# Head order, row transfers and mid-slot products in the scans of a hybrid encoder kernel

## The reference

```python
seg = a_cs[:, :, :, None] - a_cs[:, :, None, :]      # cumulative sums, position l minus position s
decay = jnp.exp(jnp.where(lower, seg, -jnp.inf))
cb = jnp.einsum('bclgn,bcsgn->bclsg', Cc, Bc)
y_diag = jnp.einsum('bclsge,bcsgep->bclgep', cb[..., None] * decay, X)
...
y_off = jnp.einsum('bclgn,bcgepn->bclgep', Cc, s_in) * jnp.exp(a_cs)[..., None]
return (y_diag + y_off).reshape(b, s, h, p)
```

## Time and profile before

| | |
|---|---|
| time, 3 runs | 1684.62 us median (1684.27 to 1687.24) |
| profiled execution: own time | 1684.64 us |
| profiled execution: span, first to last instruction | 1682.9 us |
| TensorE busy | 1659.0 us, 99% of the span |
| VectorE busy | 1001.9 us, 60% |
| GpSimd busy | 687.4 us, 41% |
| ScalarE busy | 679.8 us, 40% |
| granted TensorE clock | 1.00 (2.4 GHz) over the run |

### The profile page before, as it was taken

One profiled execution on the slowest core, in us unless ns is written; L12 is line 12 of the kernel. 1 busy time (PEld: TensorE's weight loads), 2 busy tenths in 40 slices (PEclk: granted clock), 3 DMA queues, 4 the chain that ended last, 5 costly groups with the idle time before them and its releaser, 6 DMA issues.

```text
span 1682.9 us, 20420 instructions
## 1 busy us (share of the span) xinstructions
PE 1659.0 (99%) x8004; PEld 1316.8 (78%) x8004; DVE 1001.9 (60%) x1387; ACT 679.8 (40%) x932; POOL 687.4 (41%) x339
## 2 busy tenths in 40 slices
PE   7999999999999999999999999999999999999999
PEld 5777787878778888888877777788777788888887
DVE  5589859778774545422236898596788654545100
ACT  5445553344443333332244555533543433333221
POOL 3432223233445555554443222232334455555443
PEclk9999999999999999999999999999999999999999
DMA  5532111212223232322224221112123223222233
GB/s 167 129 96 74 62 63 63 76 63 64 87 88 100 88 100 88 100 92 94 91 88 126 85 73 63 63 63 76 63 66 96 89 88 100 89 100 90 93 99 107
DMA packets 43231, 147.34 MB, mean 88 GB/s; under 512 B 5152, under 2 KB 5920, under 8 KB 43136
## 3 DMA queue, kind: packets, MB, share of 16 engines
q1 hardware_dynamic: 42752, 145.28, 26.9%
q0 software_dynamic: 384, 0.75, 0.4%
HBM read 143.17 MB, written 2.85 MB: 87 GB/s over the span
## 4 chain that ended last, share of the span: by engine, by line
PE 89%; DVE 6%; issue 2%; ACT 1%; POOL 1%; DMA 0%; SPq 0%; DVEq 0%
PE banks L1080 27%; PE banks L1082 26%; PE banks L1081 26%; PE banks L1172 2%; PE banks L1151 2%; PE banks L1160 2%; PE banks L1255 1%; DVE sb_w_lo L747 1%; PE banks L1268 1%; PE banks L1227 1%; PE banks L1131 1%; DVE sb_e L822 1%; PE banks L1241 1%; PE banks L1211 0%; DVE sb_squares L735 0%
## 5 line engine op out<-in xcount | busy, mean ns | idle before, releaser
L360 POOL TENSOR_TENSOR sb_w_lo<-sb_w_raw,sb_w_hi 128x1024 fp32r<-128x1024 f32 x202 | 490.4, 2428 | 633.1 <-ACT sb_w_hi L453 633.1
L1080 PE MATMUL banks<-sb_h_hi,sb_w_hi 128*128 128x512 f32 x1360 | 558.2, 410 | 16.1 <-POOL sb_w_lo L360 10.7
L453 ACT ACTIVATE sb_w_hi<-sb_w_raw 128x1024 fp32r<-128x1024 f32 x258 | 272.6, 1057 | 671.4 <-PE banks L1082 665.1
L1082 PE MATMUL banks<-sb_h_hi,sb_w_lo 128*128 128x512 f32 x1360 | 537.3, 395 | 0.0
L1081 PE MATMUL banks<-sb_h_lo,sb_w_hi 128*128 128x512 f32 x1360 | 537.1, 395 | 0.0
L1080 PEld LDWEIGHTS banks<-sb_h_hi,sb_w_hi 128*128 128x128 f32 x1360 | 256.5, 189 | 99.5 <-issue 36.9
L1081 PEld LDWEIGHTS banks<-sb_h_lo,sb_w_hi 128*128 128x128 f32 x1360 | 256.9, 189 | 61.8 <-issue 6.9
L1082 PEld LDWEIGHTS banks<-sb_h_hi,sb_w_lo 128*128 128x128 f32 x1360 | 256.5, 189 | 60.1
L1045 DVE TENSOR_TENSOR banks<-banks,sb_rstd 128x512 f32<-128x512 f32 x88 | 61.5, 699 | 144.0 <-PE banks L1082 135.7
L1080 PE MATMUL banks<-sb_ff_hi,sb_w_hi 128*128 128x512 f32 x352 | 138.9, 395 | 0.0
L1082 PE MATMUL banks<-sb_ff_hi,sb_w_lo 128*128 128x512 f32 x352 | 138.9, 395 | 0.0
(11 more groups left out here) (199 smaller groups left out, 2326.9 us busy)
## 6 DMA issues: line engine op xcount, KB each, us to landing
sb_w_raw<-w_in SPq DMA_DIRECT2D x88, 512.0 KB, 3.4
sb_w_raw<-w_up SPq DMA_DIRECT2D x88, 512.0 KB, 3.3
sb_w_raw<-w_out SPq DMA_DIRECT2D x32, 512.0 KB, 3.4
sb_w_raw<-w_down SPq DMA_DIRECT2D x32, 512.0 KB, 3.3
sb_bias_t<-bias_rows SPq DMA_DIRECT2D x16, 448.0 KB, 6.0
sb_w_raw<-w_down SPq DMA_DIRECT2D x16, 384.0 KB, 3.0
sb_x_stream<-x_t SPq DMA_DIRECT2D x4, 512.0 KB, 6.7
out_t<-sb_x_stream SPq DMA_DIRECT2D x8, 256.0 KB, 3.5
```

Of the source, the lines that this page charges most:

```text
L360: g.tensor_tensor(WLO[:, n % 2, :], W[:, n % 2, :], WHI[:, n % 2, :].bitcast(F32), ALU.subtract).then_inc(w_lo.handle, 1)
L453: sc.activation(WHI[:, n % 2, :], W[:, n % 2, :], ACT.Copy).then_inc(w_hi.handle, 1)
L1080: mm(out, whi, hhi, start=start, stop=False)
L1082: return mm(out, wlo, hhi, start=False, stop=stop)
```

## The change

The head's rows of cumulative sums no longer come from TensorE. ScalarE writes the sums and their exponentials (`exp_rows`) once a layer, SyncE stores both in DRAM (`store_rows`), and for every head a transfer spreads the two rows over 128 partitions straight into the head's tile (`head_rows`, 512 KB). Two transfers a pair fill `EA` (`pair_exps`, 2 x 192 KB), in place of ScalarE's L606. `seg` becomes eight instructions of 128 columns, each with a per-partition scalar, that subtract and limit at once, SBUF to SBUF. `CB` moves from SBUF into banks 2 and 3. The head tiles become four. GpSimd adds the directions for every head, so `within` has 8 matmuls. The tables change: the second group begins in slot 13; `SEG_AT` puts the first three heads of a group one to three slots behind its start and the others five to nine (before: three to ten); `WEIGH_AT` weighs them two to nine slots behind it; pairs stand in slots 7, 9, 11, 12 and 18, 20, 22, 24 (before 7, 9, 11, 13 and 19, 21, 23, 25), in the middle of the slot's matmuls except the fourth, which stays at its end, and `combine` follows `seg` in the slot, ahead of the slot's evacuation, except for the fourth. Two gates on GpSimd move a slot earlier or later.

```diff
-GROUP_AT = (2, 14)
-ROWS_AT = {GROUP_AT[h // 8] + 3 + h % 8: h for h in range(SSD_HEADS)}
-PAIR_AT = {GROUP_AT[t // 4] + 5 + 2 * (t % 4): t for t in range(SSD_HEADS // 2)}
+GROUP_AT = (2, 13)
+SEG_AT = {GROUP_AT[h // 8] + h % 8 + (1 if h % 8 < 3 else 2): h for h in range(SSD_HEADS)}
+WEIGH_AT = {GROUP_AT[h // 8] + 2 + h % 8: h for h in range(SSD_HEADS)}
+PAIR_AT = {GROUP_AT[t // 4] + 4 + 2 * (t % 4) + (t != 3): t for t in range(SSD_HEADS // 2)}
...
-    HEAD_E = (E[:, 0, :, :], E[:, 1, :, :], SQ[:, :, :])
+    HEAD_E = (E[:, 0, :, :], E[:, 1, :, :], rm["e_third"][:, :, :], SQ[:, :, :])
...
+    CB = BANK[:, 2:4, :]
...
+        def store_rows():
+            sp.wait_ge(*cs_row.at(1))
+            sp.dma_start(sum_rows[0, :, :], T[0:2 * DIR, 0, :]).then_inc(rows_stored.handle, 16)
+            sp.wait_ge(*cs_exp.at(1))
+            sp.dma_start(sum_rows[1, :, :], ER[0:2 * DIR, :]).then_inc(rows_stored.handle, 16)
+
+        def head_rows(h):
+            grp, n = h // 8, h % 8
+            if h == 0:
+                sp.wait_ge(*rows_stored.at(32))
+                sp.wait_ge(*at_pv.at(UNITS))
+            if n % 4 == 3:
+                sp.wait_ge(*st_mm.at(6 * grp + 6))
+            if h >= 4:
+                sp.wait_ge(*y_mm.at(2 * ((h - 4) // 2) + 2))
+            rows = bass.AP(sum_rows.tensor, h * SEQ, [[0, P], [DIR * SEQ, 2], [1, SEQ]])
+            sp.dma_start(head_e(h), rows).then_inc(rows_landed[h % 4].handle, 16)
+
+        def pair_exps(t):
+            if t >= 2:
+                sp.wait_ge(*y_read.at(t - 1))
+            for d in range(2):
+                rows = bass.AP(sum_rows.tensor, (2 * DIR + DIR * d + 2 * t) * SEQ + (P, 0)[d], [[SEQ, 2], [0, 64], [1, SEQ - P]])
+                sp.dma_start(EA[:, t % 2, d, :], rows).then_inc(ea_landed[t % 2].handle, 16)
...
+                slot = pos - POS["sc", 0]
+                if slot == 4:
+                    store_rows()
+                if slot - 2 in SEG_AT:
+                    head_rows(SEG_AT[slot - 2])
+                if slot - 1 in PAIR_AT:
+                    pair_exps(PAIR_AT[slot - 1])
...
-                if s in ROWS_AT and ROWS_AT[s] % 2 == 0:
-                    add_directions(ROWS_AT[s])
-                if s in PAIR_AT:
+                if PAIR_AT.get(s, 3) != 3:
                     add_backward(PAIR_AT[s])
+                if s in WEIGH_AT:
+                    add_directions(WEIGH_AT[s])
...
-                    act.wait_ge(*seg_read.at(h + 1))
-                    if h >= 4:
-                        act.wait_ge(*y_read.at(h // 2 - 1))
-                    sc.activation(EA[half, (h // 2) % 2, :, :].rearrange("p d l -> p (d l)"),
-                                  BANK[half, 2:4, :].rearrange("p b s -> p (b s)")[:, P:P + 768], ACT.Exp).then_inc(ea_done.handle, 1)
...
         def seg(h):
-            v.tensor_tensor(head_e(h).rearrange("p d (c l) -> p d c l", l=P),
-                            BANK[:, 2:4, :].rearrange("p d (c l) -> p d c l", l=P), columns, ALU.subtract).then_inc(seg_read.handle, 1)
-            dve.wait_ge(*seg_read.at(h + 1))
-            v.tensor_scalar(head_e(h), head_e(h), 80.0, None, ALU.min).then_inc(seg_done.handle, 1)
+            dve.wait_ge(*rows_landed[h % 4].at(16 * (h // 4 + 1)))
+            for d in range(2):
+                for c in range(QT):
+                    at = slice(P * c, P * c + P)
+                    ins = v.tensor_scalar(head_e(h)[:, d, at], head_e(h)[:, d, at], AS[:, c, column(d, h):column(d, h) + 1], 80.0,
+                                          ALU.subtract, ALU.min)
+            ins.then_inc(seg_done.handle, 1)
...
-        def row_sums(h):
...
-            for d in range(2):
-                ins = mm(bank(2 + d), SEL[:, column(d, h):column(d, h) + 1].to_broadcast([P, P]), CS[:, :], start=True, stop=True)
...
-                for h, d in ((2 * t, 0), (2 * t + 1, 0), (2 * t + 1, 1)):
+                for h in (2 * t, 2 * t + 1):
```

More of the change, by code:

```diff
@@ L233, in build_trunk @@
     x_stored = sem("x_stored")
-    sel_done, eps_done = sem("sel_done"), sem("eps_done")
+    eps_done = sem("eps_done")
+    rows_stored = sem("rows_stored", 32)
+    rows_landed = [sem(f"rows_landed{i}", 64) for i in range(4)]
+    ea_landed = [sem("ea_landed0", 128), sem("ea_landed1", 128)]
     bias_mm, bias_row = sem("bias_mm"), sem("bias_row")
@@ L270, in head_e @@
     def head_e(h):
-        return HEAD_E[h % 8 % 3]
+        return HEAD_E[h % 4]
     def par(col, n=1):
@@ L855, in state_in @@
                 return
-            if grp:
-                dve.wait_ge(*t_read.at(4))
+            dve.wait_ge(*(t_read.at(4) if grp else rows_stored.at(32)))
             col = 64 + column(d, 8 * grp)
@@ L954, in _ @@
                     dve.sem_inc(cs_col.handle, 1)
-                if s in ROWS_AT:
-                    seg(ROWS_AT[s])
+                if s in SEG_AT:
+                    seg(SEG_AT[s])
+                if PAIR_AT.get(s, 3) != 3:
+                    combine(PAIR_AT[s])
                 for grp in range(SSD_GROUPS):
@@ L1103, in block_of, with pair, between, tile @@
                 ins.then_inc(w_used.handle, 1)
-        def tile(kind, i, width=P, head=None):
+        def pair(s):
+            if s in PAIR_AT:
+                from_states(PAIR_AT[s])
+                within(PAIR_AT[s])
+        def between(s):
+            if PAIR_AT.get(s) != 3:
+                pair(s)
+        def tile(kind, i, width=P, slot=None):
             for k in range(KT):
-                if k == KT // 2 and head is not None:
-                    row_sums(head)
+                if k == KT // 2 and slot is not None:
+                    between(slot)
                 block_of(kind, i, k, width)
@@ L1270, in from_states, with output_first @@
             ins.then_inc(yo_mm.handle, 1)
-        def output_first(m, head):
+        def output_first(m, slot):
             s, b = weights("o1", m), tile_bank("o1", m)
             for k in range(KT):
-                if k == KT // 2 and head is not None:
-                    row_sums(head)
+                if k == KT // 2:
+                    between(slot)
                 at = slice(P * k, P * k + P)
@@ L1345, in _ @@
                 if kind == "o1":
-                    output_first(i, ROWS_AT.get(s))
+                    output_first(i, s)
                 else:
-                    tile(kind, i, head=ROWS_AT.get(s))
+                    tile(kind, i, slot=s)
                 if s == 0:
@@ L1364, in _ @@
                             chunk_state(6 * grp + 2 * (s - GROUP_AT[grp] - 1) + j)
-                if s in PAIR_AT:
-                    from_states(PAIR_AT[s])
-                    within(PAIR_AT[s])
+                if PAIR_AT.get(s) == 3:
+                    pair(s)
                 if s == 26:
```

78 lines of the change are left out of this document (26 added, 52 removed).

## The result

The changed kernel takes 1697.49 us (median of 4 runs, 1695.71 to 1698.76), the kernel before 1684.46 us in the runs beside it. The ratio is 1.0075, 95% interval 1.0062 to 1.0088: 13 us slower, where 1679 was forecast and 1695 was the upper end of the range.

What follows compares the result with a forecast made beforehand. TensorE (99% busy) was taken as the bound, VectorE close behind; of 17.1 us a layer new stalls left 2.9, 5.8 for two layers, from 1684.64 to 1679 us. Range 1658 to 1695; forecast alone 1674 to 1684.

Steps and rivals of the forecast that it cites:

- the 17.1 us that it can give: TensorE's most per layer: 7.5 us of row sums, 7.0 of products within chunks, 2.6 of stalls.
- A second term: Layer gain taken as 2.9 us, the middle between 0.5 by VectorE's list and 5.3 with `seg` at 1.2.
- The list itself: VectorE's work and waits followed through both groups' slots, with TensorE's resulting stalls: a layer wins 0.5 us.
- TensorE's side: In the scans: row sums gone, `within` about 1.02 us a pair, TensorE's busy share near 92%.
- VectorE's terms: For each head on VectorE: `seg` 1.6 us, `weigh` 1.2, and about 1.1 behind a GpSimd sum holding the port.
- The upper bound for `seg`, 1.8: Eight 128-column instructions on VectorE at 1.8 us, fixed part as in the 0.16 us of a one-column instruction.
- The stalls: TensorE idle for VectorE's low parts at slots 7, 11, 18 and 22, and before the fourth pair for GpSimd.
- The rows: Heads' row transfers land at 6.0 us, mostly hidden; VectorE waits 3 us at head 3 and head 11.
- The rival of late rows: Rows landing at 9.9 us lengthen waits at heads 3, 11, 5 to 7, 13 to 15: 1703; decides at 7.5; chance 0.14.
- The forecast's last sign of being wrong: The prediction is wrong if VectorE's waits in the scans are mostly for transfers.
- the 4.2 to 9.9 of the earlier trace: Landing times in us of the nearest recorded transfers, 448 KB bias transfers, median 6.0, taken for the heads' rows.
- The second forecast wait that mattered: First group's fourth pair: its products, ready at 313.7, wait for head 7's GpSimd sum at 317.7 and stand 4 us.

Runs made afterwards that it cites:

- runs with fillings: Matmuls nobody reads put before TensorE's long waits: on the changed kernel 1688.93 us; on the changed kernel with the three moves 1672.05 us.
- the third experiment: Changed kernel with row transfers of heads 3, 5, 7 and 11, 13, 15 asked for one slot earlier: 1685.5 us, 1.0006 against the kernel before.
- the three moves: Changed kernel with rows earlier, SiLU ahead of the head's exponential, head 7's (15's) sum ahead of the backward sum on GpSimd: 1681.15 us, 0.9983.
- the best run: The three moves on the changed kernel, plus matmuls nobody reads before four of TensorE's remaining waits: 1672.05 us, 0.9924 against the kernel before.

## Why the prediction was wrong

**The step that failed: that the gain of a layer is the 17.1 us that it can give, less the length of the new stalls.** The sum priced a stall at its own length, and all work at the clock of before, 1.00. The runs showed that a stall here costs its length and, mostly, a stretch at half clock behind it: 6.8 us in the first layer and 7.4 in the second, 14.3 us in all. No rival had it. Both runs with fillings show it directly: 8.6 us with the schedule as it was, 9.1 in the best one.

**A second term was too good.** The list itself gave 0.5 us a layer. The forecast took 2.9, half-way to the 5.3 that `seg` at 1.2 us would give (by its own terms, 0.5 and eleven times 0.4, that is 4.9). `seg` measured 1.58, so the 2.4 us a layer on top of the list, 4.8 in all, had no ground. The list alone says 1683.6; with the 14.3 us of the clock it is 1697.9, where 1697.5 was measured.

**TensorE's side held.** Row sums are gone, `from_states` takes 1.43 us and `within` 1.02 at full clock, as forecast. The busy share in the scans, forecast near 92%, is 88% and 92% in the two windows, slow matmuls counted as busy.

**VectorE's terms held.** `seg` 1.58 us (1.6), `weigh` 1.13 (1.2), a sum in front of `seg` or of the taps 1.03 (1.1). The Trainium skill, "SBUF — State Buffer", on who interferes with whom, has the pair of ports as an exclusive lock; the trace agrees also where the short instructions stand back to back: the 2.69 us above. The upper bound for `seg`, 1.8, was too high, and so was the estimate of the same size worked out from the Trainium skill, "VectorE: DVE Perf Modes", in the section on the TRN2 errata; the short instructions cost 0.20 us each, and eight less than the two long ones before.

**The stalls: the sum held, partly by luck; their places didn't all.** Forecast and measured in the first layer, us:

| | slot 7 | slot 11 | fourth pair | slot 18 | slot 22 | slot 24 | sum |
|---|---|---|---|---|---|---|---|
| forecast | 2.9 | 1.9 | 4.0 | 3.3 | 2.0 | 2.2 | 16.3 |
| measured | 2.73 | 1.41 | 4.63 (0.29 more for states) | 3.10 | 3.95 | 0 | 16.1 |

Slot 22 was delayed by head 13's rows, on top of SiLU: VectorE waited 3.94 us for them, its `seg` started at 386.24, ScalarE's exponential ended 2.7 us later, and SiLU, its tables and the high part followed. The part that wasn't in the forecast took that from slot 24. That the sums agree within 0.2 us is luck in part: rows came later than forecast, and with the rows on time (the third experiment) the same list of stalls is 11.5 us, 4.8 less than forecast.

**The rows: mechanism right, size and places off.** Waits were forecast at heads 3 and 11, 3 us each (3.53 and 2.69 measured). The rival of late rows put more at heads 5 to 7 and 13 to 15, from a landing at 9.9 us. The median is 5.3, so by its own condition (7.5) it didn't apply; yet single transfers land at 10, and 7.4 us of waits at heads 5, 7 and 13 came with them. The forecast had no term for the `EA` transfers that go out 5 to 9 us before these. The forecast's last sign of being wrong, VectorE waiting mostly for transfers, comes near: 13.6 us of VectorE's 35.3 us of waits in the two windows are for rows, more than for any other single cause. A landing is not one number: the 4.2 to 9.9 of the earlier trace rows was the better guide than its median.

**The second forecast wait that mattered was right in kind**: the fourth pair for GpSimd (4.0; 4.63). With earlier rows it is 3.69, with the backward sum behind it as well 2.70; with sums for even heads alone it is nothing.

**What stays open.** Not every wait was followed by a slow stretch. With the three moves 2.74 us at slot 7 was not in the first layer and was in the second; 1.78 and 1.81 us were in the first layer of two runs, and 3.40 was not in the second layer of another. So between 1.8 and 3.4 us neither the length nor the schedule alone decides, and what does wasn't isolated. What made the rows of heads 5, 7 and 13 late wasn't tested either. Of the 17.1 us a layer the best run should keep 17.1 - 10.5 = 6.6 by the forecast's list, and it is 6.1 better than before. Nor was it measured whether any one of its three moves could be left out.

## To carry to other kernels

When a change turns an engine that never stood into one that stands for a few microseconds here and there, price each wait at its length plus what TensorE's clock may take afterwards (here some 1.5 us each, 2.3 to 2.8 behind the longest), and look at the granted clock in windows of 2 us: busy shares hide it. Filling work in front of known waits gave 9 us here; only the earlier rows gave more. A wait behind a late engine's list isn't removed by taking one item from its front: follow the list to the next slots, and test moves together as well as alone.

## What the runs showed of the hardware that was not expected

- In these scans TensorE's waits of 1.8 to 4.6 us were mostly followed, or in the case of the longest already accompanied (0.54 in 318 to 320, the wait ending at 320.09), by a granted clock of 0.50. At slot 7 the clock was still 1.00 when work restarted at 268.92; from 270.43 on matmuls started 0.43 us apart, and in 274 to 276 the clock was 1.00 again.
- The same wait in the same place did and didn't: 2.74 us at slot 7 with the three moves, clock 1.00 behind it in the first layer and 0.57 in the second.
- A matmul of 512 columns then starts every 0.43 us instead of 0.23.
- Spare matmuls in front of the wait kept the clock at 1.00 behind it at each of the places where they were tried (four places in each of two runs; no slow stretch followed them).
- Transfers that spread one row over 128 partitions, 512 KB each, land in 5.0 to 11.1 us, median 5.3: no worse in the median than the 6.0 of those before, in which the partitions read different addresses, in spite of all partitions reading the same row.
